# A two-layer hybrid model step on one core: where the output pieces stand in the linear-attention stage, and which engine copies its level products

## The chip, the cores and the metric

The kernel runs on one core of one Trainium2 chip. The metric is the device time of one execution in microseconds, from the first to the last instruction on the core and what lies around it. The engines are TensorE (PE, with its weight loads PEld), VectorE (DVE), ScalarE (ACT), GpSimd (POOL) and SyncE (SP), which issues most DMAs. All arithmetic here is in 32-bit floats.

## The reference

The model takes 1024 prompt tokens and 8 x 4 sample tokens through two layers. Each layer has a token mixer (pooling, latent attention and gated linear attention side by side, joined by `w_out`), cross attention, and a mixture of experts. The change touches the linear attention of the mixer, and the product with `w_out` that is begun beside it:

```python
def gla(q, k, v, log_a, s0):                       # 4 heads, DK 32, DV 64
    def step(S, inp):                              # one chunk of tokens
        qb, kb, vb, gb = inp
        b = jnp.cumsum(gb, axis=2)
        o_inter = jnp.einsum('bhtk,bhkv->bhtv', qb * jnp.exp(b), S)
        decay = jnp.exp(jnp.where(causal, b[:, :, :, None, :] - b[:, :, None, :, :], -jnp.inf))
        att = jnp.einsum('bhtsk,bhsk->bhts', qb[:, :, :, None, :] * decay, kb)
        o_intra = jnp.einsum('bhts,bhsv->bhtv', att, vb)
        S = jnp.exp(b_last)[..., None] * S + jnp.einsum('bhsk,bhsv->bhkv', kb * jnp.exp(b_last - b), vb)
        return S, o_inter + o_intra

y = jnp.concatenate([ya, yb, yc], axis=-1) @ lw['w_out']   # pooling, latent, linear attention
x = x + y
```

## The kernel before, in words

The program is written out by hand: every engine has its own list of instructions, and semaphores with counts order them. Each layer is a row of stages with a barrier (`stage_end`, L479) behind most. The third stage, "stage 3" here, is the linear attention: L1036 to L1141 on TensorE, L1723 to L1786 on ScalarE, L2210 to L2350 on VectorE, L2821 to L2856 on GpSimd. It stands once in each layer, behind the latent attention (stage 2), whose head pairs 0 to 3 use two weight slots `w_h` in turn.

Stage 3 works on 8 tiles of 128 tokens. Positions of a tile that are paired by the causal mask are split into 7 levels: at level z (64, 32, ..., 1) the first half of each block of 2z positions meets the second half. For tile n:

- VectorE `begin(n)` (L2219): a running sum of the log decays (L2225), then 7 subtractions (L2229), one for each level. There are two buffers, used in turn by even and odd tiles.
- ScalarE `decay_exps(n)` (L1726, L1727) takes exponentials of those, `state_exps(n)` (L1733 to L1735) those for the state.
- GpSimd multiplies them with q and k, 14 short products (L2834, L2836) and three longer (L2839, L2841, L2842). Count 2n+1 of `g_pool` stands for L2839, the last that the level products need.
- TensorE `levels(n)` (L1044, L1045): 28 small products into PSUM banks 0 to 3, one buffer only.
- VectorE `take_levels(n)`: 7 masked copies of them to the attention tile `g_att` (L2239), and a product for the diagonal (L2240), which counts `at_free`.
- TensorE `turn_kt` (L1051), `outputs` (L1058, L1060), `states` (L1067), and later `turn_o` (L1076) for the transposed outputs.
- VectorE `add_state` (L2261, a product with the mask of the 4 diagonal blocks, and L2262), `take_o` (L2247), `norm_o` for two tiles at a time (L2253, L2256, L2257).

Eight pieces of the product with `w_out` (`part(i)`, L1086: 6 contraction steps of 352 columns, in one PSUM bank, 5) are put between these on TensorE. VectorE adds each to x (`add_part`, L2269), and piece i + 1 waits for that (`part_or_counts_ready`). Their weights come in the four `ring` slots, which stage 2 uses for its probabilities, so that SyncE loads them behind the barrier. `keep_clock` (L760) issues products of constants that nothing reads. Behind the eight tiles the stage does the same for the 32 sample tokens (L2298 to L2345 on VectorE, L1112 to L1141 on TensorE).

Times in this section's stage are read from the execution's start: stage 3 begins at 423.97 us in layer 0 and at 1717.24 us in layer 1.

## Time and profile before

| | |
|---|---|
| median of 3 runs | 2597.96 us (2595.11 to 2601.43) |
| the profiled execution's own time | 2599.04 us |
| its span | 2597.2 us |
| PE busy | 2401.4 us, 92% |
| DVE busy | 1143.3 us, 44% |
| ACT busy | 689.8 us, 27% |
| POOL busy | 468.2 us, 18% |
| stage 3, layer 0 | 423.97 to 522.63 us |
| stage 3, layer 1 | 1717.24 to 1815.9 us |

A row of a timeline has the start in us, the duration in us, the engine, the line, the operation, what it writes and reads, and how many such instructions in a row it stands for; in brackets how long the engine sat idle before it, and what ended that. A duration of "x7" is that of all seven. A row of windows has the busy time and number of instructions of each engine in that stretch, then TensorE's granted clock as a share of 2.4 GHz, and the DMA load.

### The profile page before, as it was taken

How to read it: one execution, taken by the hardware profiler on the slowest of the kernel's cores; microseconds unless marked ns; L12 is line 12 of the kernel's file. 1: busy time of each engine (PE TensorE's matmuls, PEld its weight loads, DVE VectorE, ACT ScalarE, POOL GpSimd, SP SyncE). 2: the span in 40 equal slices, each digit the busy share in tenths (PEclk: the TensorE clock that was granted, in tenths of full speed). 3: DMA queues.
4: the chain of work that ended last, by engine and by line, in shares of the span. 5: the costliest groups of instructions: out<-in, count | busy, mean ns of one | idle time of the engine just before them, and what ended most of it. 6: DMA issues, size and time to landing. Idle time of an engine off the chain costs nothing.

```text
span 2597.2 us, 38234 instructions
## 1 busy us (share of the span) xinstructions
PE 2401.4 (92%) x15944; PEld 1422.5 (55%) x15944; DVE 1143.3 (44%) x2122; ACT 689.8 (27%) x1452; POOL 468.2 (18%) x566
## 2 busy tenths in 40 slices
PE   8999998899999999999899999888989999999984
PEld 5645556666666765333366445566666676733332
DVE  3355556843241445333253555568431433633334
ACT  1034444432111331111130344544321123311113
POOL 6004223410100001111260042243100000011112
PEclk9999999999999999999999999999999999999996
DMA  5001001152224228999840010011522421589996
GB/s 187 11 19 30 11 5 38 42 197 92 89 90 148 82 90 310 396 422 422 333 141 11 19 30 11 5 38 44 205 82 65 149 82 65 198 345 406 424 418 244
DMA packets 79220, 389.31 MB, mean 150 GB/s; under 512 B 20654, under 2 KB 24364, under 8 KB 59532
## 3 DMA queue, kind: packets, MB, share of 16 engines
q1 hardware_dynamic: 60892, 308.07, 31.1%
q0 software_dynamic: 17568, 76.57, 7.6%
q8 instruction: 131, 2.15, 0.3%
q10 hardware_dynamic: 576, 2.10, 0.2%
q14 instruction: 53, 0.43, 0.1%
HBM read 354.53 MB, written 41.41 MB: 152 GB/s over the span
## 4 chain that ended last, share of the span: by engine, by line
PE 73%; DVE 11%; ACT 4%; issue 4%; DMA 3%; PEld 2%; POOL 1%; POOLq 0%; PEldq 0%; SPq 0%; DVEq 0%; ACTq 0%
PE ps L1494 12%; PE ps L784 8%; PE ps L807 8%; PE ps L1518 6%; PE ps L1404 4%; PE ps L875 4%; PE ps L955 4%; PE ps L967 3%; PE ps L983 2%; PEld ps L807 2%; PE ps L1160 2%; PE ps L933 2%; DVE arena L2239 2%; PE ps L1480 2%; DMA arena<-yrow 1%
## 5 line engine op out<-in xcount | busy, mean ns | idle before, releaser
L1494 PE MATMUL ps<-arena 128*32 128x512 f32 x2304 | 319.6, 608 | 24.6 <-issue 18.9
L807 PE MATMUL ps<-arena,ring 128*128 128x352 f32 x936 | 283.2, 466 | 1.0 <-ACTq L481 1.0
L784 PE MATMUL ps<-x,ring 128*128 128x352 f32 x768 | 231.5, 463 | 10.6 <-DMA x<-in_x 9.1
L807 PEld LDWEIGHTS ps<-arena,ring 128*128 128x128 f32 x936 | 180.4, 193 | 101.9 <-issue 4.3
L2683 DVE COPY arena<-ps 128x1024 f32<-128x1024 f32 x44 | 53.9, 1224 | 336.9 <-PE ps L1480 336.9
L1494 PEld LDWEIGHTS ps<-arena 128*32 128x32 f32 x2304 | 92.7, 112 | 191.4 <-issue 191.4
L784 PEld LDWEIGHTS ps<-x,ring 128*128 128x128 f32 x768 | 146.8, 192 | 92.7 <-issue 12.8
L1518 PE MATMUL ps<-arena 128*32 128x512 f32 x1408 | 160.2, 595 | 3.8 <-ACT arena L1914 3.8
L2883 POOL DMA_INDIRECT arena<-xrow,arena x46 | 46.8, 1017 | 594.8 <-DVE arena L2658 321.3
L955 PE MATMUL ps<-arena 96*128 96x512 f32 (+3 forms) x384 | 148.7, 497 | 0.0
L1680 ACT ACTIVATE ring<-ps 128x512 f32<-128x512 f32 (+2 forms) x192 | 87.3, 490 | 128.7 <-PE ps L967 128.6
L1404 PE MATMUL ps<-arena,ring 128*128 128x352 f32 x384 | 117.7, 463 | 1.6 <-DVE arena L2516 1.6
L1160 PE MATMUL ps<-consts,arena 128*128 128x128 f32 x640 | 100.6, 297 | 18.9 <-ACT arena L1795 9.6
L875 PE MATMUL ps<-arena,x 128*128 128x512 f32 x256 | 114.5, 608 | 2.2 <-ACT arena L1628 2.2
L1494 PE MATMUL ps<-ring,arena 128*32 128x512 f32 x512 | 114.3, 600 | 0.0
L967 PE MATMUL ps<-consts,ring 128*128 128x128 f32 x576 | 91.4, 287 | 24.7 <-DVE arena L2151 9.7
L1685 ACT ACTIVATE ring<-ps,nmax 128x128 f32<-128x128 f32 (+7 forms) x128 | 94.5, 740 | 54.6 <-DVE nmax L2141 54.1
L1909 ACT ACTIVATE arena<-ps 128x256 f32<-128x256 f32 x44 | 16.9, 383 | 334.8 <-PE ps L1494 334.8
L2139 DVE TENSOR_TENSOR ps<-ps,consts 128x128 f32<-128x128 f32 x128 | 38.3, 299 | 150.2 <-PE ps L955 149.3
L1160 PEld LDWEIGHTS ps<-consts,arena 128*128 128x128 f32 x640 | 74.5, 150 | 48.9 <-ACT arena L1795 19.9
L2140 DVE TENSOR_REDUCE nmax<-ps 128x1 f32<-128x128 f32 (+7 forms) x128 | 97.0, 758 | 4.4
L967 PEld LDWEIGHTS ps<-consts,ring 128*128 128x128 f32 x576 | 65.6, 144 | 58.4 <-issue 35.1
(471 smaller groups left out, 3836.3 us busy)
## 6 DMA issues: line engine op xcount, KB each, us to landing
arena<-in_w_gu SPq DMA_DIRECT2D x52, 2048.0 KB, 14.3
arena<-in_w_dn SPq DMA_DIRECT2D x64, 1024.0 KB, 11.4
ring<-in_ring SPq DMA_DIRECT2D x56, 512.0 KB, 3.7
ring<-in_w_gu SPq DMA_DIRECT2D x12, 2048.0 KB, 13.7
arena<-yrow SPq DMA_DIRECT2D x16, 1024.0 KB, 9.3
arena<-in_mem_k SPq DMA_DIRECT2D x16, 512.0 KB, 7.6
arena<-in_mem_v SPq DMA_DIRECT2D x16, 512.0 KB, 9.5
xrow<-arena SPq DMA_DIRECT2D x16, 512.0 KB, 7.7
```

What stands on the lines that cost most here:

```text
L784: mm = pe.matmul(ps[:, PIECE_BANKS[n % len(PIECE_BANKS)], 0:CH], ring[:, j % RING, k, :], x[:, k, tok], start=k == 0, stop=k == KT - 1)
L807: mm = pe.matmul(ps[:, (j % 2) * NCH + c, 0:CH], ring[:, j // per, (j % per) * units + k, :], src[:, k, tok], start=k == k0, stop=k == uni ...
L875: mm = pe.matmul(ps[:, 6 + t % 2, :], x[:, k, t * P:t * P + m], wvg[:, k, :], start=k == 0, stop=k == KT - 1)
L955: mm = pe.matmul(ps[:, bank + at // 512, 0:end - at], q_h[0:QK, b, qb * P:(qb + 1) * P], k_h[0:QK, b, at:end], start=True, stop=True)
L967: mm = pe.transpose(ps[:, bank, (kb % 4) * P:(kb % 4 + 1) * P], prob[:, e, kb * P:(kb + 1) * P], ident)
L1160: mm = pe.transpose(ps[:, turn_bank(u), j * P:(j + 1) * P], b, ident)
L1404: mm = pe.matmul(ps[:, (j % 2) * NCH + c, 0:CH], ring[:, slot, (j % 2) * XH + k, :], co[:, k, tok], start=k == 0, stop=k == XH - 1)
L1494: mm = pe.matmul(ps[r, 2 + n % 2, :], xb_t[:, n % 2, k, r], w_gu[e % NW][:, k, :], start=k == 0, stop=k == KT - 1, skip_group_check=True)
L1518: mm = pe.matmul(ps[r, 4 + f, :], h_t[:, k, r], w_dn[e % NW][:, k, f * 512:(f + 1) * 512], start=k == 0, stop=k == 1, skip_group_check=True)
L1680: act.activation(pt[:, e, 512 * half:512 * half + w], ps[:, 4 + m % 2, 0:w], ACT.Copy).then_inc(tp_free[m % 2], 1)
L1685: act.activation(prob[:, e, 0:w], ps[:, 2 * e:2 * e + 2, :].rearrange("p a n -> p (a n)")[:, 0:w], ACT.Exp, bias=nmax[:, e, 1:2], scale=ML ...
L2140: step(dve.reduce_max(nmax[:, e, 0:1], sc, AX))
```

## The change

Four edits, all in stage 3.

1. **Pieces.** SyncE loads the weights of pieces 0 and 1 (both use the same block of `w_out`) during the last pair of stage 2, into the slot that pair 2 has left (`w_first`, a view of `w_h[0]`). TensorE does pieces 0 and 1 at the start of the stage in place of 10 `keep_clock` products, piece 2 behind `levels(0)`, and the rest behind tiles 0, 1, 2, 3 and 5. In place of piece 7 behind the tiles stand 16 `keep_clock` products; the 14 in tile 0 go.
2. **Levels.** Levels 64, 32 and 16 are copied by ScalarE with 7 unmasked copies, `keep_levels(n)`, which wait for `at_free` and count `at_kept`; VectorE keeps 4 masked copies. `levels` and `outputs` on TensorE wait for `at_kept` too.
3. **State.** The state product is written as 4 products of 32 x 64, one for each head, into diagonal blocks of a bank that VectorE has zeroed once; the masking product L2261 goes.
4. **Order.** VectorE does `begin(2)` ahead of the tiles, behind a wait for `g_pool`, and `add_part(0)` and `add_part(1)` behind it. GpSimd waits for `at_done` from tile 2 on.

```diff
@@ SyncE
+                sp.wait_ge(tp_done, SLOT[PAIRS - 2, ("a", 1, 0)] + 1)
+                sp.dma_start(w_first, ins["ring"][l, 2 * RING + PART[0][0]][:, 0:PART_K, :]).then_inc(w_full[0], 16)
@@ TensorE
                     if n >= 1:
                         pe.wait_ge(at_free, n)
+                        pe.wait_ge(at_kept, n)
...
-                    pe.matmul(ps[:, 7, 0:GW], g_ktt[:, n % 2, :], vg[:, n, 0:GW], start=True, stop=True).then_inc(st_done, 1)
+                    for h in range(GH):
+                        r, v = slice(GK * h, GK * (h + 1)), slice(GV * h, GV * (h + 1))
+                        mm = pe.matmul(ps[r, 7, v], g_ktt[:, n % 2, r], vg[:, n, v], start=True, stop=True)
+                    mm.then_inc(st_done, 1)
...
-                keep_clock(5, 10)
                 part(0)
+                part(1)
                 levels(0)
-                part(1)
+                part(2)
...
-                    if n == 0:
-                        pe.wait_ge(part_or_counts_ready, 2)
-                        keep_clock(5, 14)
-                    if 1 <= n <= len(PART) - 3:
-                        part(1 + n)
+                    if n in PART_AT:                       # (0, 1, 2, 3, 5)
+                        part(3 + PART_AT.index(n))
...
-                part(len(PART) - 1)
+                keep_clock(5, 16)
@@ ScalarE
+                def keep_levels(n):
+
+                    act.wait_ge(at_free, n + 1)
+                    for lv, z in enumerate(LEVELS[:HIGH]):
+                        for b in range(HALF // z):
+                            s_, at = 2 * z * b, lv * HALF + z * b
+                            last = act.activation(g_att[s_:s_ + z, n % 2, :, s_ + z:s_ + 2 * z], ps[s_:s_ + z, 0:GH, at:at + z], ACT.Copy)
+                            if at + z < HIGH * HALF:
+                                step.mark(last)
+                    last.then_inc(at_kept, 1)
...
+                decay_exps(2)
+                keep_levels(0)
                 for n in range(NT):
-                    if n + 2 < NT:
+                    if n >= 1 and n + 2 < NT:
                         decay_exps(n + 2)
...
+                    if n + 1 < NT:
+                        keep_levels(n + 1)
                     head_squares(n, P)
@@ VectorE
-                    for lv, z in enumerate(LEVELS):
+                    for lv, z in list(enumerate(LEVELS))[HIGH:]:
...
-                    step(dve.tensor_tensor(g_tmp, ps[:, bank, 0:GW], bd, ALU.mult))
-                    dve.scalar_tensor_tensor(out=dst, in0=dst, scalar=scale, in1=g_tmp, op0=ALU.mult, op1=ALU.add).then_inc(st_ready, 1)
+                    dve.scalar_tensor_tensor(out=dst, in0=dst, scalar=scale, in1=ps[:, bank, 0:GW], op0=ALU.mult, op1=ALU.add).then_inc(st_ready, 1)
...
+                step.mark(dve.memset(ps[:, 7, 0:GW], 0.0))
+                step.sync()
                 dve.memset(state, 0.0).then_inc(st_ready, 1)
                 begin(0)
-                begin(1)
                 step.mark(dve.memset(d_e[:, 2, :], 1.0))
                 step(dve.memset(g_att, 0.0))
+                begin(1)
+                dve.wait_ge(g_pool, 1)
+                begin(2)
                 add_part(0)
+                add_part(1)
...
-                add_part(len(PART) - 1)
@@ GpSimd
+                    if n >= 2:
+                        pool.wait_ge(at_done, n - 1)
                     pool.wait_ge(g_exp, 2 * n + 1)
```

How VectorE's list begins in stage 3, before (L2225 and L2229 are `begin`, L2269 is `add_part`, L2239 the first masked copy of tile 0; names in brackets are the semaphores waited for):

```order
L2271 MEMSET arena 128x256 [waits stage_done]
L2225 SCALAR_TENSOR_TENSOR arena<-arena 128x128
...
L2225 SCALAR_TENSOR_TENSOR arena<-arena 128x128
...
L2229 TENSOR_TENSOR arena<-arena 128x64x2
L2274 MEMSET arena 128x32
L2275 MEMSET arena 128x1024
L2269 TENSOR_TENSOR x<-x,ps 128x352 [waits part_or_table_done,dve_step]
L2239 COPY_PREDICATED arena<-lmask,ps 128x4x64 [waits at_done]
```

And now (L2248 and L2252 are `begin`, L2291 is `add_part`, L2262 the first masked copy):

```order
L2293 MEMSET ps 128x256 [waits stage_done]
L2295 MEMSET arena 128x256 [waits dve_step]
L2248 SCALAR_TENSOR_TENSOR arena<-arena 128x128
...
L2298 MEMSET arena 128x1024
L2248 SCALAR_TENSOR_TENSOR arena<-arena 128x128 [waits dve_step]
...
L2248 SCALAR_TENSOR_TENSOR arena<-arena 128x128 [waits g_exp,g_pool]
...
L2252 TENSOR_TENSOR arena<-arena 128x64x2
L2291 TENSOR_TENSOR x<-x,ps 128x352 [waits part_or_table_done] x2
L2262 COPY_PREDICATED arena<-lmask,ps 128x32x8 [waits at_done]
```

A third `begin`, with a wait for GpSimd, has moved in front of the addition of piece 0.

How TensorE's list begins in stage 3, before (L760 is `keep_clock`, L1086 a piece, L1044 and L1045 `levels`):

```order
L760 MATMUL ps<-consts 128x128 [waits stage_done]
L760 MATMUL ps<-consts 128x128 x9
L1086 MATMUL ps<-arena,ring 128x352 [waits ring_full1]
L1086 MATMUL ps<-arena,ring 128x352 x5
L1044 MATMUL ps<-arena 128x64 [waits g_pool,g_zero]
L1044 MATMUL ps<-arena 128x64 x27
L1045 MATMUL ps<-consts,arena 128x4
L1086 MATMUL ps<-arena,ring 128x352 [waits part_or_counts_ready,ring_full1]
```

And now (L1098 is a piece, L1049 and L1050 are `levels`):

```order
L1098 MATMUL ps<-arena 128x352 [waits pair_or_gu_full,stage_done]
L1098 MATMUL ps<-arena 128x352 x5
L1098 MATMUL ps<-arena 128x352 [waits part_or_counts_ready,pair_or_gu_full]
L1098 MATMUL ps<-arena 128x352 x5
L1049 MATMUL ps<-arena 128x64 [waits g_pool,g_zero]
L1049 MATMUL ps<-arena 128x64 x27
L1050 MATMUL ps<-consts,arena 128x4
L1098 MATMUL ps<-arena,ring 128x352 [waits part_or_counts_ready,ring_full2]
```

Piece 1, which waits for the addition of piece 0, has moved in front of the level products of tile 0.

ScalarE's list for one tile without square roots, now (L1735 and L1736 are `decay_exps`, L1748 `take_kt`, L1742 to L1744 `state_exps`, L1756 `keep_levels`, L1765 `head_squares`):

```order
L1735 ACTIVATE arena<-arena 128x7x64 [waits g_sub]
L1736 ACTIVATE arena<-arena 128x7x64
L1748 ACTIVATE arena<-ps 128x128 [waits kt_done]
L1742 ACTIVATE arena<-arena 128x128 [waits st_ready]
L1743 ACTIVATE arena<-arena 128x128
L1744 ACTIVATE arena<-arena 128x1
L1756 ACTIVATE arena<-ps 64x4x64 [waits at_free]
L1756 ACTIVATE arena<-ps 32x4x32 x2
L1756 ACTIVATE arena<-ps 16x4x16 x4
L1765 ACTIVATE arena<-arena 128x64 [waits o_evac]
```

Before, the list is the same without the three rows of L1756: they stand now behind the exponentials that wait for the state.

## Rows read from the trace of the kernel before

**Rows 1.** Windows: us, busy per engine, granted clock, DMA; tiles of layer 0.

```profile
434.51:500.71 66.20, 60.11 (x644) 47.43 (x644) 62.30 (x157) 27.00 (x106) 40.21 (x118) 1.00 0.08 29
```

**Rows 2.** Timeline, all engines, start of stage 3 in layer 0.

```profile
423.97 1.80 POOL L2821 MEMSET arena<- 128x2048 f32 x1 [53.25 <-DVEq L481]
424.09 0.27 DVE L2271 MEMSET arena<- 128x256 f32 x1 [0.23 <-DVEq L481]
...
427.56 0.47 POOL L2834 TENSOR_TENSOR arena<-arena 128x64 f32<-128x64 f32 x1
...
431.76 0.46 POOL L2839 TENSOR_TENSOR arena<-arena 128x128 f32<-128x128 f32 x1
...
432.37 1.79 PE L1044 MATMUL ps<-arena 32*128 32x64 f32 x56 [0.89 <-POOL arena L2839]
...
434.51 3.86 DVE L2239 COPY_PREDICATED arena<-lmask,ps 128x256 f32<-128x256 uint8 x7 [2.40 <-PE ps L1045]
```

**Rows 3.** Timeline, tile 1 to tile 2 of layer 0, and first copies of tiles 5, 6.

```profile
441.12 3.86 DVE L2239 COPY_PREDICATED arena<-lmask,ps 128x256 f32<-128x256 uint8 x7
442.08 0.90 DVE L2239 COPY_PREDICATED arena<-lmask,ps 128x256 f32<-128x256 uint8 x2
...
445.35 0.42 DVE L2261 TENSOR_TENSOR arena<-ps,consts 128x256 f32<-128x256 f32 x1
...
445.80 0.52 DVE L2262 SCALAR_TENSOR_TENSOR arena<-arena 128x256 f32<-128x256 f32 x1
...
446.35 0.31 ACT L1733 ACTIVATE arena<-arena 128x128 f32<-128x128 f32 x1 [3.88 <-DVE arena L2262]
...
446.57 0.41 DVE L2225 TENSOR_TENSOR_SCAN arena<-arena 128x128 f32<-128x128 f32 x1
...
446.95 0.24 ACT L1745 ACTIVATE arena<-arena 128x64 f32<-128x64 f32 x1
447.01 2.19 DVE L2229 TENSOR_TENSOR arena<-arena 128x128 f32<-128x128 f32 x7
...
447.28 1.79 PE L1044 MATMUL ps<-arena 32*128 32x64 f32 x56 [0.94 <-POOL arena L2839]
...
449.43 3.86 DVE L2239 COPY_PREDICATED arena<-lmask,ps 128x256 f32<-128x256 uint8 x7 [0.22 <-PE ps L1045]
...
449.82 1.00 PE L1060 MATMUL ps<-arena 128*128 128x64 f32 x8
...
451.15 3.71 PE L1086 MATMUL ps<-arena,ring 128*128 128x352 f32 x12
...
454.96 1.79 PE L1044 MATMUL ps<-arena 32*128 32x64 f32 x56
...
471.80 0.60 PE L1076 MATMUL ps<-consts,arena 128*128 128x128 f32 x4
...
476.19 3.83 DVE L2239 COPY_PREDICATED arena<-lmask,ps 128x256 f32<-128x256 uint8 x7
...
486.46 3.84 DVE L2239 COPY_PREDICATED arena<-lmask,ps 128x256 f32<-128x256 uint8 x7
```

**Rows 4.** Groups by line: busy us, mean ns of one; ScalarE's copies out of PSUM.

```profile
L1909 ACT ACTIVATE arena<-ps 128x256 f32<-128x256 f32 x44 | 16.9, 383 | 334.8 <-PE ps L1494 334.8
L1739 ACT ACTIVATE arena<-ps 128x128 f32<-128x128 f32 x8 | 2.1, 257 | 0.0
```

**Rows 5.** Windows of 1 us in stage 3 of layer 0; the clock stands third from last.

```profile
427.00:428.00 1.00, 1.00 (x9) 0.96 (x9) 1.00 (x6) 1.00 (x4) 0.87 (x3) 0.97 1.01 406
509.00:510.00 1.00, 0.69 (x2) 0.29 (x2) 0.93 (x4) 0.00 (x0) 0.00 (x0) 0.50 0.00 0
```

**Rows 6.** Timeline, tile 7 and what follows it, layer 0.

```profile
493.04 3.85 DVE L2239 COPY_PREDICATED arena<-lmask,ps 128x256 f32<-128x256 uint8 x7 [0.67 <-PE ps L1045]
...
500.71 0.42 DVE L2261 TENSOR_TENSOR arena<-ps,consts 128x256 f32<-128x256 f32 x1 [0.17 <-PE ps L1067]
...
507.60 0.84 PE L1114 MATMUL ps<-arena 128*32 128x128 f32 x6 [2.93 <-DVE arena L2321]
```

More of the change, by code:

```diff
@@ L106 @@
 PART = ((1, 1), (1, 0), (2, 0), (2, 1), (3, 0), (3, 1), (0, 0), (0, 1))
+PART_AT = (0, 1, 2, 3, 5)
 PART_K = 6
@@ L254, in build @@
         w_h = [view(SC + 4128, WP), view(SC + 256, WP)]
+        w_first = view(SC + 4128, PART_K, P)
         q_dec = view(SC, DB, ND)
@@ L271, in build @@
         la_t = view(SC + 3072 + TOK, TOK)
-        NL = len(LEVELS)
+        NL, HIGH = len(LEVELS), 3
         HALF = P // 2
@@ L388, in build @@
         g_sub, g_exp, g_pool, g_dve = sem("g_sub"), sem("g_exp"), sem("g_pool"), sem("g_dve")
-        at_done, at_free = sem("at_done"), sem("at_free")
+        at_done, at_free, at_kept = sem("at_done"), sem("at_free"), sem("at_kept_or_rx_in")
         kt_done, kt_evac, st_done, st_ready = sem("kt_done"), sem("kt_evac"), sem("st_done"), sem("st_ready")
@@ L407, in build @@
         wr_full, lg_done, lg_evac, lt_done = sem("wr_full"), sem("lg_done"), sem("lg_evac"), sem("lt_done")
-        rx_in, rx_out = sem("rx_in"), sem("rx_out")
+        rx_in, rx_out = at_kept, sem("rx_out")
         ranked, routed = sem("ranked"), sem("routed")
@@ L413, in build @@
         row_moved = [sem(f"row_moved{j}") for j in range(4)]
-        wg_full = [(sem(f"wg_full{j}"), 0) for j in range(4)] + [(w_full[0], 16 * PAIRS // 2)]
+        wg_full = [(sem(f"wg_full{j}"), 0) for j in range(4)] + [(w_full[0], 16 * (PAIRS // 2 + 1))]
         wd_full = [(s, 32 * PAIRS) for s in swap_or_dn_full] + [(w_full[1], 16 * PAIRS // 2)]
@@ L1050, in turn_kt @@
                     pe.wait_ge(st_ready, n + 1)
-                    pe.transpose(ps[:, 7, 0:P], g_kt[:, n % 2, :], ident).then_inc(kt_done, 1)
+                    pe.transpose(ps[:, 7, GW:GW + P], g_kt[:, n % 2, :], ident).then_inc(kt_done, 1)
                 def outputs(n):
                     pe.wait_ge(at_free, n + 1)
+                    pe.wait_ge(at_kept, n + 1)
                     if n >= 1:
@@ L1081, in part @@
                     j, c = PART[i]
-                    pe.wait_ge(ring_full[j], ring_count(l, 3))
+                    if i <= 1:
+                        pe.wait_ge(w_full[0], 16 * (PAIRS // 2 + 1))
+                    else:
+                        pe.wait_ge(ring_full[j], ring_count(l, 3))
                     if i >= 1:
@@ L1085, in part @@
                     for k in range(PART_K):
-                        mm = pe.matmul(ps[:, 5, 0:CH], ring[:, j, k, :], mix[:, k, chunks[c][1]], start=k == 0, stop=k == PART_K - 1)
+                        mm = pe.matmul(ps[:, 5, 0:CH], w_first[:, k, :] if i <= 1 else ring[:, j, k, :], mix[:, k, chunks[c][1]], start=k == 0, stop=k == PART_K - 1)
                     mm.then_inc(part_or_table_done, 1)
-                keep_clock(5, 10)
                 part(0)
+                part(1)
                 levels(0)
-                part(1)
+                part(2)
                 for n in range(NT):
@@ L1119, in _ @@
                 pe.wait_ge(st_ready, NT + 1)
-                pe.transpose(ps[0:ND, 7, 0:P], g_kt[:, 0, 0:ND], ident).then_inc(kt_done, 1)
+                pe.transpose(ps[0:ND, 7, GW:GW + P], g_kt[:, 0, 0:ND], ident).then_inc(kt_done, 1)
                 pe.wait_ge(ds_full, 16 * GH)
@@ L1900, in _ @@
                                    scale=rstd_t[0:m, t:t + 1]).then_inc(xr_evac, 1)
-                act.wait_ge(rx_in, 1)
+                act.wait_ge(rx_in, NT + 1)
                 act.activation(r_exp, r_exp, ACT.Exp).then_inc(rx_out, 1)
@@ L2213, in _ @@
                 hm = con("headmask").unsqueeze(2)
-                bd = con("bdmask")
                 def split(a, z):
@@ L2280, in _ @@
                     if n == 0:
-                        add_part(1)
+                        add_part(2)
                     if n >= 1:
@@ L2285, in _ @@
                         take_o(n - 1)
-                    if n + 2 < NT:
+                    if n >= 1 and n + 2 < NT:
                         begin(n + 2)
@@ L2290, in _ @@
                         norm_o(n - 2, P)
-                    if 2 <= n <= len(PART) - 2:
-                        add_part(n)
+                    if n - 1 in PART_AT:
+                        add_part(3 + PART_AT.index(n - 1))
                 dve.wait_ge(st_done, NT)
```

4 lines of the change are left out of this document (2 added, 2 removed).

## The prediction

> **What bounds the kernel now.** The page's busy shares say TensorE (92%), but they average over stages, and the change lies in one stage of each layer. So I read that stage. Over the eight tiles of layer 0, 66.20 us, VectorE is busy 62.30 us and TensorE 60.11 us [rows 1]: both are nearly full, and VectorE is the fuller. Next the timeline of two tiles. Tile 1's masked copies begin at 441.12, tile 2's at 449.43, 8.31 us later, and VectorE has sat idle only 0.22 us [rows 3]. Tiles 5 and 6, between which two tiles are normalised, lie 486.46 - 476.19 = 10.27 us apart with no idle time named [rows 3]. So the tiles run at VectorE's pace. Two others are close behind. On TensorE the level products of consecutive tiles, with a piece between, begin at 447.28 and 454.96: 7.68 us, and the latter with no wait in front [rows 3]. And those at 447.28 had waited 0.94 us for GpSimd. The start of the stage has another bound: a chain VectorE, ScalarE, GpSimd, TensorE that gives the first level products at 432.37, while piece 0 is done beside it [rows 2].
>
> I count from the stage's start, 423.97. T0 to T7 are the starts of VectorE's masked copies of each tile. Before: T0 = 434.51 - 423.97 = 10.54 [rows 2], T1 = 17.15, T5 = 52.22 and T6 = 62.49 [rows 3], T7 = 69.07, and the last state addition begins at 76.74 [rows 6].
>
> **The start: pieces 0 and 1, and begin(2).** The intended gain is that piece 0 needs no ring slot and takes the place of products that nobody reads. Those stood in time that TensorE had to wait anyway, for GpSimd's L2839 (ends 431.76 + 0.46 = 432.22, [rows 2]). What matters is the new order. TensorE now does piece 1 ahead of the level products of tile 0; piece 1 waits for the addition of piece 0; and VectorE does that behind begin(2), which waits for GpSimd's first tile. Step by step, from the stage's start:
> - A PSUM memset with its own wait comes ahead of begin(0). The like in the arena is 0.27 [rows 2]; with the wait I take 0.3.
> - GpSimd's tile 0 ran from 427.56 to 432.22, that is 3.59 to 8.25 [rows 2]. It shifts by 0.3. Begin(1) now lies beside its products, which slows some of them (the first is 0.47, with VectorE busy; the fourteen span 4.20 in all, 0.30 each): 0.4 to 0.8 more. I take 9.2.
> - begin(2): 0.41 + 2.19 = 2.6, the price beside a busy GpSimd [rows 3]: 11.8. The addition of piece 0, about 0.5 (as long as L2262, 0.52, [rows 3]): 12.3.
> - Piece 1 begins at 12.35. Piece 0 ended near 5.3 (its 3.71 [rows 3] and the slow clock of the first 3 us: the first window at 0.97 is that of 427, [rows 5]). TensorE has been idle for 7 us. After the idle 2.93 us in front of 507.60 [rows 6] and short work behind it the clock was 0.50 at 509 [rows 5]. So I expect 1.2 GHz for the first 3 us of piece 1 at least, which adds half of that, 1.5: piece 1 ends at 12.35 + 3.71 + 1.5 = 17.6.
> - The level products to the first copy took 434.51 - 432.37 = 2.14 [rows 2]: T0 = 19.7. That is 9.2 later than before. Bounds: 6.4 (GpSimd at 8.4, begin(2) at 1.9, full clock) and 10.6 (slower GpSimd, slow clock into the level products too).
>
> What hides here: the third begin and its exponentials are done, so nothing of tile 2 is late. Between T0 and T1 the order is copies, ScalarE, level products 1; before, 441.12 - 434.51 = 6.61. Now 2.9 + 1.2 + 2.2 = 6.3 with the prices below: 0.3 less. T1 = 26.0, before 17.15.
>
> **The levels.** Seven copies take 3.86; the fourth starts about 0.45 behind 442.08, at 442.53, so the first three, those that go, cost 1.41 and four cost 2.45 [rows 3]. The mask product goes too: 445.80 - 445.35 = 0.45 [rows 3]. VectorE saves 1.86 a tile, 14.9 over eight. If VectorE still set the pace, tiles would take 8.3 - 1.9 = 6.4, and with norms 10.3 - 1.9 = 8.4. But two bounds stop that.
>
> ScalarE's seven copies have no row here. The three shapes are 256, 128 and 64 elements out of PSUM. One of 256 is 0.383, one of 128 is 0.257 [rows 4]. Consecutive ScalarE instructions overlap by about 0.1 (0.31 starting at 446.35 and two more are over by 446.95, [rows 3]). Upper bound: 0.38 + 6 x 0.26 = 1.9 without overlap. Lower: 0.3 + 6 x 0.1 = 0.9. I take 1.2, near 0.28 + 2 x 0.16 + 4 x 0.14.
>
> The chain from tile to tile: copies 2.45, diagonal product to its end 0.45 (at_free at 2.9), state addition until 3.3, ScalarE's three exponentials 446.95 - 446.35 = 0.6 [rows 3] to 3.9, keep_levels 1.2 to 5.1, then level products to the next copy 449.43 - 447.28 = 2.15 [rows 3]: 7.3. It exists because keep_levels stands behind the exponentials that wait for the state, and the level products have one PSUM buffer.
>
> TensorE: with a piece in the tile 7.68, as before. The state product is 8 instructions of 64 columns instead of two of 256. The eight of this width in outputs take 1.00, from 449.82 to 450.82, and the state product then takes what is left until the piece at 451.15, some 0.3 to 0.5 [rows 3]. So it costs between nothing and 0.6 more. I take 0, since its products are 32 columns wide and one eighth of the size. The Trainium skill (TensorE: Matmul & The Clock Gate, Part 3: Packing small matmuls) says that products whose outputs start at different groups of 32 partitions run beside each other. No row here shows it for four groups; the upper bound of 0.6 in five tiles would make the sum 3 us a layer higher, the rule leaves it as it is.
>
> So tiles with a piece take 7.7: T1 to T3 15.4. T3 to T4 has norms and a piece to add: VectorE, 8.4 (10.27 - 1.86). T5 = T3 + 16.0 (TensorE 2 x 7.7 and 0.60 for the turned outputs, the row of 471.80, [rows 3]). T5 to T6, norms, no piece: 8.2. T6 to T7: TensorE has a piece and turned outputs behind its level products of tile 6: T7 = T5 + 15.6. Sum T1 to T7 47.0; before 51.92. So 4.9 is gained of the 11.2 that VectorE loses in six tiles. In T5 to T6 TensorE idles some 3 us without its piece; that may drop the clock, at a price of 0 to 1.5 in the tile behind: 0.7.
>
> T7 to the last state addition: before 500.71 - 493.04 = 7.67 [rows 6]. Now copies 1.4 shorter, but keep_levels(7) 1.2 in front of outputs(7), and keep_clock and the roots as before: 6.9, 0.8 less. Behind it, 16 constant products stand where piece 7 stood: TensorE waits for VectorE there anyway (2.93, [rows 6]). The addition of piece 7, behind which the last norms stood, goes: 0.4 less. The extra DMA of SyncE (weights of pieces 0 and 1) falls into stage 2, where nothing waits for it; it costs nothing; were it late, piece 0 would still come before GpSimd's first tile is done. The pool's wait for at_done of tile n - 2 is met long before; nothing.
>
> **Sum.** A layer: +9.2 - 0.3 - 4.9 + 0.7 - 0.8 - 0.4 = +3.5. Two layers: +7.0. The profiled execution, 2599.04, becomes 2606.0; it lies 1.1 above the median of the runs, whose sum would be 2605.0. I say 2605.5.
>
> At one more place the Trainium skill prices what I bounded: VectorE: DVE Perf Modes, The TRN2 errata, has a ScalarE copy out of PSUM at 172 cycles and one per element at 1.2 GHz, and ScalarE: Activation LUTs (What ACT_TABLE_LOAD costs) has consecutive ones overlap by about 93 ns. By that, an estimate, 128 elements are 0.25, where [rows 4] has 0.257, and the seven copies are 1.15. The sum would be 0.1 a layer lower.
>
> **Rivals.** A measurement of this kernel can tell 0.2%, 5.2 us, from no change.
>
> *The loss and the gain cancel (chance 0.20).* GpSimd's first tile is not slowed, begin(2) takes 1.9, the clock comes back early: T0 6.6 to 7.5 later, and the tiles gain 6. A layer +0.5 to +1.5, 2598 to 2602, say 2600. For it: in the first 3 us the chip came back to full clock within that time [rows 5]. Against: begin beside a busy GpSimd has been 2.6 each time.
>
> *ScalarE becomes the pace (0.18).* The seven copies cost nearer 1.9, on partial partitions, and stand behind table loads in even tiles; the chain from tile to tile is 8.0 to 8.3, and only 1 to 2 us of VectorE's saving is left. The clock is low in more tiles. A layer +6.5 to +8.5: 2613. For it: ScalarE's load in these tiles is only 27.00 of 66.20 [rows 1], so it is a matter of latency alone; against it the durations of [rows 4].
>
> *Faster (0.08).* VectorE sets the pace to the end: chain and TensorE overlap better than I have it, tiles take 6.4 and 8.4, the full 14.9 come off, against 9.2 at the start: -5.7 - 0.4 a layer, -12, 2587. It decides where the tiles with a piece fall below 7.0 us. Against it speaks TensorE's own 7.68 with no idle time [rows 3]; only fewer pieces in the tiles (five instead of six) speaks for it.
>
> The forecast itself has 0.54, with its own range of +2 to +5.5 a layer, 2602 to 2610. It covers 0.06 below 5.2 us of change. So slower by over 0.2% has 0.48 + 0.18 and some of the first rival's upper edge: 0.68; within 0.2% 0.23; faster 0.09. The range that leaves out no more than 2 in 10 goes from 2597.5 to 2614.
>
> **What would show it.** In the changed kernel's trace: piece 1 begins 11 to 13.5 us behind the stage's start, TensorE idle for 5 us or more in front of it, ended by the addition of piece 0; its granted clock at 0.50 there. First masked copy at 17 to 21 instead of 10.54. Tiles 1 to 3 apart by 7.3 to 8.0, TensorE without idle time or waiting for ScalarE's copies, VectorE with idle time in every tile. The last state addition 2 to 6 us later than 76.74. It would be wrong if piece 1 started before 9, or if tiles were apart by under 7, or if the time changed outside stage 3.

## The result and the profile after

The changed kernel takes 2610.05 us (median of 12 runs, 2603.2 to 2620.27), the kernel before 2597.22 on the same chip (12 runs, 2587.59 to 2603.88). The ratio is 1.0052, 95% interval 1.004 to 1.0064: 0.4 to 0.6% slower, some 13 us. The forecast was 2605.5, range 2597.5 to 2614. Direction and range held; the loss is 12.8, where the forecast stood for +7.5. One execution below, of e6_state_only, fell into a slow state (4095.66 us) and is left out.

First the page of the changed kernel: its span and the busy share of each engine.

```profile
span 2607.1 us, 38430 instructions
PE 2399.9 (92%) x16008; PEld 1423.2 (55%) x16008; DVE 1126.0 (43%) x2060; ACT 717.3 (28%) x1564; POOL 469.4 (18%) x566
```

VectorE has 17.3 us less to do than before (1143.3) and ScalarE 27.5 more (689.8); the span is longer all the same. So less work did not help; where it stands has to be looked at. Stage 3 of layer 0 now runs from 418.12 to 528.07, 109.95 us instead of 98.66; in layer 1 109.78 instead of 99.11 (in the kernel before that stage ends at 1816.35, where TensorE begins the next one, not at 1815.9).

The start of the stage on TensorE, changed kernel (timeline; against [rows 2]):

```profile
418.12 5.33 PE L1098 MATMUL ps<-arena 128*128 128x352 f32 x12 [1.53 <-DVEq L483]
430.66 5.87 PE L1098 MATMUL ps<-arena 128*128 128x352 f32 x12 [7.21 <-DVE x L2291]
436.46 1.79 PE L1049 MATMUL ps<-arena 32*128 32x64 f32 x56
...
443.45 1.80 PE L1049 MATMUL ps<-arena 32*128 32x64 f32 x56 [1.23 <-ACT arena L1756]
...
448.83 5.33 PE L1098 MATMUL ps<-arena,ring 128*128 128x352 f32 x12
454.10 1.79 PE L1049 MATMUL ps<-arena 32*128 32x64 f32 x56
```

Piece 0, then 7.21 us of nothing, ended by VectorE's addition (L2291), then piece 1, 5.87 instead of 3.7. The level products of tile 0 come only behind it, at 18.3 us from the stage's start; in [rows 2] they began at 8.4. VectorE's side of the same wait:

```profile
427.06 0.66 DVE L2248 TENSOR_TENSOR_SCAN arena<-arena 128x128 f32<-128x128 f32 x1 [2.32 <-POOL arena L2867]
427.75 2.41 DVE L2252 TENSOR_TENSOR arena<-arena 128x128 f32<-128x128 f32 x7
430.00 0.51 DVE L2291 TENSOR_TENSOR x<-x,ps 128x352 f32<-128x352 f32 x1
```

It sits idle for GpSimd, does begin(2), and only then adds piece 0, which had been ready since about 423.4.

The tiles on VectorE (first masked copy of tiles 0, 1, 2, then 5, 6, 7, and the last state addition; against [rows 3, 6]):

```profile
438.60 2.44 DVE L2262 COPY_PREDICATED arena<-lmask,ps 128x256 f32<-128x256 uint8 x4 [1.51 <-PE ps L1050]
445.80 2.41 DVE L2262 COPY_PREDICATED arena<-lmask,ps 128x256 f32<-128x256 uint8 x4 [3.03 <-PE ps L1050]
...
456.24 2.44 DVE L2262 COPY_PREDICATED arena<-lmask,ps 128x256 f32<-128x256 uint8 x4 [1.51 <-PE ps L1050]
...
480.93 2.43 DVE L2262 COPY_PREDICATED arena<-lmask,ps 128x256 f32<-128x256 uint8 x4 [1.45 <-PE ps L1050]
...
490.85 2.42 DVE L2262 COPY_PREDICATED arena<-lmask,ps 128x256 f32<-128x256 uint8 x4 [1.44 <-PE ps L1050]
...
501.39 2.42 DVE L2262 COPY_PREDICATED arena<-lmask,ps 128x256 f32<-128x256 uint8 x4 [1.95 <-PE ps L1050]
...
508.06 0.48 DVE L2284 SCALAR_TENSOR_TENSOR arena<-arena,ps 128x256 f32<-128x256 f32 x1 [1.06 <-PE ps L1075]
```

VectorE, which had no idle time to speak of in [rows 3], now waits for TensorE's level products in front of nearly every tile: it sets the pace no more. The tiles did not come closer for it: T1 to T2 is 10.44 (8.31 before), T5 to T6 9.92 (10.27), T6 to T7 10.54 (6.58). Windows of the changed kernel, where the granted clock stands third from last, show why two of these are long:

```profile
437.00:445.00 8.00, 6.77 (x117) 5.12 (x110) 3.36 (x7) 1.66 (x7) 4.38 (x15) 1.00 0.01 2
445.00:452.00 7.00, 7.00 (x37) 5.21 (x32) 5.72 (x15) 2.65 (x12) 1.08 (x2) 0.51 0.00 0
452.00:486.00 34.00, 28.95 (x356) 22.04 (x354) 26.73 (x68) 23.39 (x89) 20.88 (x66) 1.00 0.01 2
486.00:497.00 11.00, 9.97 (x84) 8.25 (x85) 6.81 (x18) 5.40 (x26) 7.23 (x21) 0.53 0.01 3
```

In [rows 1] the clock was 1.00 over all eight tiles. Here it is at half, 1.2 GHz, for 7 us around piece 3 and for some 10 us in tiles 5 and 6. Layer 1 of the kernel before was not free of it either: its clock fell once, for about 3.4 us in tile 1, and T1 to T2 took 8.74 there instead of 8.31:

```profile
1734.00:1738.00 4.00, 4.00 (x21) 3.64 (x19) 3.79 (x9) 1.21 (x3) 2.37 (x9) 0.57 0.00 0
```

Ahead of the changed kernel's second fall lies a gap, in the one tile without a piece; the timeline of TensorE there:

```profile
482.26 0.32 PE L1075 MATMUL ps<-arena 128*32 128x64 f32 x8
487.03 3.27 PE L1049 MATMUL ps<-arena 32*128 32x64 f32 x56 [4.45 <-ACT arena L1756]
...
493.88 5.00 PE L1098 MATMUL ps<-arena,ring 128*128 128x352 f32 x12
```

And the waits of the whole stage (engine and line, what it waited for: us in all, times, longest):

```profile
PE ps L1049 <- ACT arena L1756: 7.3, 5, 4.5
PE ps L1098 <- DVE x L2291: 7.2, 1, 7.2
```

ScalarE's seven copies, by form (busy us, mean ns of one), and in one tile behind the three exponentials:

```profile
L1756 ACT ACTIVATE arena<-ps 16x64 f32<-16x64 f32 x32 | 6.9, 214 | 0.8
L1756 ACT ACTIVATE arena<-ps 32x128 f32<-32x128 f32 x16 | 4.1, 259 | 0.2
L1756 ACT ACTIVATE arena<-ps 64x256 f32<-64x256 f32 x8 | 2.9, 364 | 11.3 <-DVE arena L2263 11.3
```

```profile
449.49 0.31 ACT L1742 ACTIVATE arena<-arena 128x128 f32<-128x128 f32 x1 [3.09 <-DVE arena L2284]
449.70 0.39 ACT L1743 ACTIVATE arena<-arena 128x128 f32<-128x128 f32 x1
450.00 0.19 ACT L1744 ACTIVATE arena<-arena 128x1 f32<-128x1 f32 x1
450.09 1.76 ACT L1756 ACTIVATE arena<-ps 64x256 f32<-64x256 f32 x7
```

The 128 and 256 forms cost what [rows 4] said (0.257 and 0.383), but the sum of the seven, 1.74, is also their time: they do not overlap, while the exponentials ahead of them do, by 0.1 (0.31 from 449.49, the next one starts at 449.70).

### The profile page after: what moved, and what is told of

It is laid out like the page before. It is cut to its first block, busy times and chain, and to the rows that moved or that the text cites. A ratio compares the mean times of both kernels' runs of the same rounds, so it can differ in the third digit from the quotient of the medians.

```text
span 2607.1 us, 38430 instructions
## 1 busy us (share of the span) xinstructions
PE 2399.9 (92%) x16008; PEld 1423.2 (55%) x16008; DVE 1126.0 (43%) x2060; ACT 717.3 (28%) x1564; POOL 469.4 (18%) x566
## 4 chain that ended last, share of the span: by engine, by line
PE 76%; DVE 10%; ACT 5%; issue 4%; PEld 2%; DMA 2%; PEldq 1%; POOL 1%; POOLq 0%; SPq 0%; DVEq 0%; ACTq 0%
PE ps L1503 12%; PE ps L788 9%; PE ps L811 8%; PE ps L1527 6%; PE ps L1413 4%; PE ps L879 4%; PE ps L959 4%; PE ps L971 2%; PE ps L987 2%; PE ps L1169 2%; PEld ps L811 2%; PE ps L937 2%; PE ps L1489 2%; PE ps L1098 1%; DVE nmax L2164 1%
## 5 line engine op out<-in xcount | busy, mean ns | idle before, releaser
L811 PEld LDWEIGHTS ps<-arena,ring 128*128 128x128 f32 x936 | 179.7, 192 | 101.3 <-issue 3.2
L788 PEld LDWEIGHTS ps<-x,ring 128*128 128x128 f32 x768 | 147.0, 192 | 92.9 <-issue 13.2
L1413 PEld LDWEIGHTS ps<-arena,ring 128*128 128x128 f32 x384 | 71.7, 190 | 46.1 <-issue 6.8
```

What stands on the lines that cost most here:

```text
L788: mm = pe.matmul(ps[:, PIECE_BANKS[n % len(PIECE_BANKS)], 0:CH], ring[:, j % RING, k, :], x[:, k, tok], start=k == 0, stop=k == KT - 1)
L811: mm = pe.matmul(ps[:, (j % 2) * NCH + c, 0:CH], ring[:, j // per, (j % per) * units + k, :], src[:, k, tok], start=k == k0, stop=k == uni ...
L1413: mm = pe.matmul(ps[:, (j % 2) * NCH + c, 0:CH], ring[:, slot, (j % 2) * XH + k, :], co[:, k, tok], start=k == 0, stop=k == XH - 1)
```

## The experiments

Stage 3 of both layers, from each kernel's one profiled execution; "rest" is the span without the two. The ratio is to runs of the kernel before on the same chip, whose medians were 2593.52 to 2597.22; compare kernels by the ratio first. A number behind T is a tile: T1 to T2 is the time from the first masked copy of tile 1 to that of tile 2.

| kernel | layer 0 | layer 1 | rest | median | ratio, 95% |
|---|---|---|---|---|---|
| before | 98.66 | 99.11 | 2399.4 | 2597.22 | |
| changed | 109.95 | 109.78 | 2387.4 | 2610.05 | 1.0052 (1.004 to 1.0064) |
| e1_add_first | 102.92 | 106.08 | 2397.4 | 2600.21 | 1.0012 (0.9993 to 1.003) |
| e2_kept_clock | 112.67 | 111.06 | 2395.7 | 2618.91 | 1.0087 (1.0061 to 1.0113) |
| e2b_kept_30 | 109.60 | 106.46 | 2395.0 | 2612.22 | 1.0072 (1.0048 to 1.0096) |
| e3_levels_dve | 110.07 | 110.06 | 2385.3 | 2607.32 | 1.0052 (1.0032 to 1.0071) |
| e4_keep_early | 109.01 | 109.35 | 2393.7 | 2615.27 | 1.0077 (1.0054 to 1.01) |
| e5_both | 100.65 | 100.80 | 2391.1 | 2598.33 | 1.001 (0.999 to 1.003) |
| e6_state_only | 96.66 | 95.64 | 2391.3 | 2588.48 | 0.9983 (0.9966 to 1.0) |
| e7_state_levels | 97.38 | 95.53 | 2388.5 | 2586.07 | 0.9971 (0.995 to 0.9991) |
| e8_fill_gap | 104.70 | 106.11 | 2384.9 | 2610.95 | 1.0059 (1.0038 to 1.008) |
| e11_one_a_tile | 93.98 | 93.95 | 2392.6 | 2583.06 | 0.9951 (0.9931 to 0.997) |
| e12_one_keep_early | 92.57 | 94.81 | 2403.3 | 2582.95 | 0.9942 (0.9922 to 0.9961) |
| e13_old_start_keep_early | 95.57 | 92.20 | 2394.4 | 2579.76 | 0.9925 (0.9901 to 0.995) |

The theory was: the new order at the start loses some 10 us a layer, and lowered clocks in the tiles eat what VectorE gains. The rival: the seven copies on ScalarE set a slower pace.

**e1_add_first**: the order at the start.

```diff
                 begin(1)
+                add_part(0)
                 dve.wait_ge(g_pool, 1)
                 begin(2)
-                add_part(0)
                 add_part(1)
```

> The changed kernel, with one line moved: VectorE adds piece 0 ahead of its wait for GpSimd and begin(2), not behind them. Theory (the new order makes TensorE wait 7 us for that addition): piece 1 begins some 6 us behind the stage's start instead of 12.5, without a slow clock; the first masked copy (T0) at about 12 us instead of 20.5, and the cold stretch in tile 1 goes with it. Stage 3 takes 99 to 102 us instead of 110.0, the kernel 16 to 22 us less than the changed one: equal to the kernel before within 0.2%. Rival (the stall is hidden by what follows; ScalarE's copies in the chain from tile to tile cost the 13 us): T0 comes earlier but the last state addition hardly moves; the kernel stays 8 us or more above the one before.

The time fell to 1.0012, which cannot be told from the kernel before, as expected. The way there was not: the first copy starts at 15.98, instead of 20.47 in the changed kernel and of the 12 expected, and piece 1, which begins at 7.11, is still slow:

```profile
434.20 6.80 PE L1098 MATMUL ps<-arena 128*128 128x352 f32 x12 [3.30 <-DVE x L2291]
```

So the position of one 0.51 us addition behind begin(2) costs some 4.5 us at the start of each layer, and the kernel 0.4%. The rest of the delay there is piece 1 itself, ahead of the level products. The fall of the clock in tile 1 is gone in layer 0 and still there in layer 1 (T1 to T2 7.94 and 10.71).

**e2_kept_clock** and **e2b_kept_30**: 60 or 30 constant products behind piece 0, so that TensorE stays busy in the gap.

```diff
                 part(0)
+                keep_clock(6, 60)
                 part(1)
```

> The changed kernel, with 60 products of constants (7 us) between piece 0 and piece 1, so that TensorE is not idle while it waits. It leaves the wait and takes away the slow clock that follows. If the clock is what costs: piece 1 takes 3.7 us instead of 5.87, and with the clock still up in tile 1 the stage is 4 to 5 us shorter in each layer, the kernel 8 to 10 us. If the wait itself costs (my theory): only the 2.1 us of piece 1 and perhaps the 2.5 us of tile 1 come back, T0 at 18.3, and the kernel stays 5 to 9 us above the one before.

> As e2 with 30 products of constants between pieces 0 and 1, about 7 us (60 took 13.56 us in e2 and pushed piece 1 back by 4.6 us). Clock alone: piece 1 begins where it does in the changed kernel (12.5 us behind the stage's start) and takes 3.7 us instead of 5.87: T0 at 18.3. If the 7.2 us of idle time are also what lets the clock fall in tile 1, both layers' T1 to T2 take 7.9 instead of 10.4: stage 3 4 to 5 us shorter, kernel 8 to 10 us less. If not (e2 had 10.7 in layer 0 and 7.94 in layer 1 there): 2 to 3 us a layer, kernel 4 to 6 us less than the changed one.

Neither is faster than the changed kernel; every branch of both expectations had them some 4 us or more below it. TensorE in e2_kept_clock, layer 0:

```profile
424.57 13.56 PE L764 MATMUL ps<-consts 128*128 128x128 f32 x120
437.97 3.71 PE L1098 MATMUL ps<-arena 128*128 128x352 f32 x12
...
453.63 5.75 PE L1098 MATMUL ps<-arena,ring 128*128 128x352 f32 x12
```

Piece 1 is back at 3.71, so its 5.87 was the clock. But 60 products last 13.56 us, not the 7 planned and longer than the gap, and the piece starts late, at 17.05. And the clock falls again around piece 3 (5.75) after 30 us in which TensorE was idle for 1.23 us at most: the later fall does not need a slow clock or a long gap before it. With 30 products (6.86 us) piece 1 begins at 12.56 as planned; it takes 5.48 in layer 0, behind 2.05 us of idle time, and 3.79 in layer 1, behind 0.36, and only in layer 1 does T1 to T2 stay at 7.94. Products that fill a gap are themselves in the way if they last longer than it.

**e3_levels_dve**: the changed kernel with all seven copies back on VectorE.

```diff
-        NL, HIGH = len(LEVELS), 3
+        NL, HIGH = len(LEVELS), 0
...
-                keep_levels(0)
```

> The changed kernel, with all seven levels copied by VectorE again; the order, the pieces and the state edit stay. Theory (sharing the levels gains nothing, since the chain through ScalarE and TensorE's pieces set the pace, and lets TensorE's clock fall): T0 stays near 20.5; T1 to T7 takes 47 to 50 us instead of 55.6 (VectorE's 51.9 of before less 0.45 a tile), and the clock stays up in the tiles. Stage 3 103 to 106 instead of 110, the kernel 6 to 14 us below the changed one. Rival (sharing is a gain that the start hides): the tiles get longer than 55.6 and the kernel slower than the changed one.

The same time as the changed kernel, and the same stage to 0.3 us a layer. With this order of pieces the sharing neither costs nor gains; the rival falls. What was expected fails too: the tiles did not get shorter (T1 to T7 56.17), and the clock fell in the same two places, so it is not the sharing that lets it fall. In this kernel, too, TensorE idles 4.29 us in the tile without a piece, there ended by GpSimd, and the level products behind it take 3.27.

**e4_keep_early**: ScalarE's copies ahead of the exponentials that wait for the state; **e5_both**: this and the order of e1.

```diff
+                    if n + 1 < NT:
+                        keep_levels(n + 1)
                     if n + 2 < NT:
                         state_exps(n + 2)
                     if n >= 2 and n % 2 == 0:
                         act.wait_ge(o_root, n // 2)
-                    if n + 1 < NT:
-                        keep_levels(n + 1)
```

> The changed kernel, with ScalarE's keep_levels(n+1) moved ahead of the exponentials that wait for the state. Theory (the copies stand in the chain from tile to tile, behind the state addition and the exponentials, and behind a second table load in even tiles): tiles bound by that chain get 1 us shorter, tile 5 to 6 some 2 us, TensorE's idle 4.45 us there becomes 2, its clock stays up and tile 6 to 7 gets 2 to 3 us shorter. Stage 3 takes 102 to 105 us instead of 110.0, the kernel 10 to 16 us less than the changed one. Rival (TensorE and its pieces set the pace of tiles, not ScalarE): under 2 us a layer.

> Both edits, the addition of piece 0 first and keep_levels early. If the stall at the start and the chain through ScalarE are separate costs they add up: stage 3 at 91 to 95 us against 98.7 before, the kernel 8 to 15 us below the one before (2583 to 2589). If they share a cost (the slow clock behind one of them is the same loss), the stage stays at 97 to 100 and the kernel within 0.2% of the one before.

e4 is not faster (1.0077; its interval overlaps that of the changed kernel), where 10 to 16 us less were expected. Tiles with a piece came 7.5 instead of 7.97 apart, but T5 to T6 stayed at 9.8, and T6 to T7 took 11.2 instead of 10.5:

```profile
490.57 3.26 PE L1049 MATMUL ps<-arena 32*128 32x64 f32 x56 [4.33 <-POOL arena L2867]
```

The gap remains, now ended by GpSimd: it seems that two chains of nearly one length end there, and taking one away shows the other. e5 is as e1 in time (1.001 against 1.0012), the second branch of its expectation; its stages, 100.7, are a little longer than the 97 to 100 named there.

**e6_state_only** and **e7_state_levels**: the kernel before with the new state product and addition (no mask product), and with these and the shared levels; pieces and start as before.

```diff
-                    pe.matmul(ps[:, 7, 0:GW], g_ktt[:, n % 2, :], vg[:, n, 0:GW], start=True, stop=True).then_inc(st_done, 1)
+                    for h in range(GH):
+                        r, v = slice(GK * h, GK * (h + 1)), slice(GV * h, GV * (h + 1))
+                        mm = pe.matmul(ps[r, 7, v], g_ktt[:, n % 2, r], vg[:, n, v], start=True, stop=True)
+                    mm.then_inc(st_done, 1)
```

> The kernel before with the state edit alone (four products of 32 x 64 into diagonal blocks of a zeroed bank, no masking product on VectorE). VectorE sets the pace there: 0.45 us less in each of eight tiles, less 0.3 for the memset and wait. Stage 3 95 to 96 us instead of 98.7, the kernel 5 to 7 us below the one before. Rival (TensorE's eight small products cost as much, or GpSimd's chain takes over): within 2 us.

> The kernel before with the state edit and the levels shared with ScalarE; its start, pieces and clock products stay. The chain copies, state addition, exponentials, ScalarE's copies (1.76), level products is 7.95 us, TensorE 7.7 with a piece: T1 to T7 48 to 50 us against 51.9. T0 stays at 10.9, but T1 comes 0.5 later. If the clock stays up (a piece in each tile 1 to 6): stage 3 95 to 97, kernel 3 to 7 us below the one before and not better than the state edit alone. If the clock falls in it too: stage 3 99 to 103, kernel above the one before; then sharing costs by itself, whatever the order at the start.

The state edit alone is at -0.17%, and its interval touches 1; the two together are a gain, 0.29%. What the sharing adds to the state edit cannot be told from nothing. In layer 0 of e7 the clock fell too (T2 to T3 10.71, against 7.96 in layer 1), and the kernel still gains. With the two parts alone the ratio is 0.9971, with the new pieces 1.0052. So the loss of the change comes with its pieces (their places, or the early weights), not with its arithmetic.

**e8_fill_gap**: 17 constant products in tile 4 of the changed kernel.

```diff
+                    if n == 4:
+                        pe.wait_ge(part_or_counts_ready, 7)
+                        keep_clock(5, 17)
```

> The changed kernel with 17 constant products (nobody reads them) in tile 4, the one tile without a piece. Theory, the gap lowers the clock: TensorE idles 4.45 us ahead of the level products of tile 5, which then take 3.27 instead of 1.79, and everything to piece 7 runs at 1.2 GHz. With the products in the gap the clock stays at 2.4 GHz: tile 5 to 6 about 8.4 us instead of 9.92, tile 6 to 7 about 8 instead of 10.54, the last state addition near 86 instead of 89.9 from the stage's start, 3.5 to 4.5 us a layer, time about 2602. Rival, ScalarE's table loads and GpSimd's late chain set these two tiles: both stay over 9.5 us and the time stays at 2608 to 2611.

In the trace the theory holds to 0.1 us: T5 to T6 8.42, T6 to T7 7.95 in layer 0, 8.41 and 7.96 in layer 1, at a clock of 1.00.

```profile
482.92 4.06 PE L764 MATMUL ps<-consts 128*128 128x128 f32 x34
487.45 1.79 PE L1049 MATMUL ps<-arena 32*128 32x64 f32 x56 [0.46 <-ACT arena L1759]
...
491.17 3.82 PE L1098 MATMUL ps<-arena,ring 128*128 128x352 f32 x12
```

The wait for ScalarE fell from 4.45 to 0.46: the products fill the gap and hold nothing up. The stages are 5.3 and 3.7 us shorter. But the median is 2610.95, as that of the changed kernel: the profiled execution (2597.53) was the fastest of eight, the other seven took 2605 to 2616. The gain of this trace does not show in the times. The fastest execution also had the highest granted clock of the eight, 0.967 on average, the others 0.962 to 0.966; whether the clock fell in tiles 5 and 6 of the others all the same, or they lost the gain elsewhere, is not in any trace.

**e11_one_a_tile**: free slot, shared levels and state product as in the change, its pieces laid out otherwise.

```diff
-PART_AT = (0, 1, 2, 3, 5)
+PART_AT = (0, 1, 2, 3, 4, 5)
...
                 part(0)
-                part(1)
+                keep_clock(6, 14)
                 levels(0)
-                part(2)
+                part(1)
...
-                        part(3 + PART_AT.index(n))
+                        part(2 + PART_AT.index(n))
...
                 begin(1)
+                add_part(0)
                 dve.wait_ge(g_pool, 1)
                 begin(2)
-                add_part(0)
-                add_part(1)
```

> The changed kernel (free slot, shared levels, new state product) with its pieces laid out otherwise: piece 0, 14 constant products, levels of tile 0, piece 1, then one piece in each of tiles 0 to 5; the addition of piece 0 stands ahead of the wait for GpSimd. Theory, the place of the pieces costs the changed kernel its gain: first masked copy at 11 to 13 us from the stage's start instead of 20.5, tiles about 8 us apart, the last state addition at 74 to 78, time 2584 to 2592, as of the kernel before with the state and level edits alone (2586.1) or a little under. Rival, the early weights and their DMA or the sharing itself cost something: the first copy stays beyond 15 and the time over 2596.

As expected: 2583.06, 0.49% under the kernel before, where the changed kernel is 0.52% over it. First copy at 11.91; T1 to T7 49.53 and 49.48, where the changed kernel took 55.59 and 55.45. TensorE at the start, and the window over the tiles:

```profile
432.25 3.29 PE L764 MATMUL ps<-consts 128*128 128x128 f32 x28
436.20 1.79 PE L1049 MATMUL ps<-arena 32*128 32x64 f32 x56 [0.66 <-POOL arena L2866]
...
438.17 3.80 PE L1098 MATMUL ps<-arena 128*128 128x352 f32 x12
```

```profile
439.04:495.56 56.52, 51.18 (x612) 38.66 (x611) 43.40 (x107) 36.01 (x143) 37.24 (x114) 1.00 0.01 2
```

The clock is 1.00 throughout. The first level products wait for GpSimd, those in the tiles for ScalarE's copies (0.41 to 0.81 us, 1.92 in front of tile 1). This separates the free slot, which is harmless, from the places of the pieces. Against e1, which has the addition of piece 0 in the same place, it is another 0.6%; it moves piece 1 behind the level products and puts a piece into tile 4 at once, and no run tells which of the two gives how much.

**e12_one_keep_early** and **e13_old_start_keep_early**: e11 and e7 with ScalarE's copies early, the edit of e4.

> As the kernel with one piece a tile, and ScalarE's copies of the next tile stand ahead of the exponentials that wait for the state. Theory, the chain from tile to tile through ScalarE binds in the tiles with a piece (TensorE waits 0.4 to 0.7 for it): tiles come 7.5 apart instead of 7.97, 2 to 3 us a layer, 4 to 5 us in all below it. Rival, TensorE's own work is 7.5 and VectorE then waits for the state: under 2 us in all.

> The kernel before with the state edit and the shared levels, its own pieces and start kept, and ScalarE's copies ahead of the exponentials. Theory, same as for the other early one: 0.4 us a tile, 2582 to 2584 against 2586.1 with the copies behind them. Rival, the state chain is delayed by as much: 2586 or more.

e12 is 2582.95, e11 2583.06: no gain that can be told, where 4 to 5 us were expected, though T1 to T7 is 46.7 in both layers. e13 is 2579.76, 0.75% under the kernel before, the best median of all; its interval (0.9901 to 0.995) meets those of e7, e11 and e12, so which of them is best is not settled. In e13, layer 1, the level products of consecutive tiles come 7.47 apart with no wait in front:

```profile
1742.54 1.79 PE L1045 MATMUL ps<-arena 32*128 32x64 f32 x56
...
1746.26 3.82 PE L1091 MATMUL ps<-arena,ring 128*128 128x352 f32 x12
1750.01 1.79 PE L1045 MATMUL ps<-arena 32*128 32x64 f32 x56
```

In these tiles TensorE is the bound at last. It was 7.68 in [rows 3].

## Why the prediction was right in sign and short in size

By its own steps, layer 0 (layer 1 in brackets), us a layer:

| step | forecast | measured |
|---|---|---|
| T0 | +9.2 | +9.93 (+9.84) |
| T0 to T1 | -0.3 | +0.59 (+0.69) |
| T1 to T7, with the clock's 0.7 | -4.2 | +3.67 (+3.01) |
| T7 to the last state addition | -0.8 | -1.00 (-1.01) |
| behind it | -0.4 | -1.90 (-1.86) |
| sum | +3.5 | +11.29 (+10.67) |

**The start** was right in mechanism and nearly in size: GpSimd's tile is done at 8.9 (9.2 forecast), begin(2) takes 2.9 (2.6), the addition of piece 0 ends the idle time, 12.54 us behind the stage's start (12.35), idle 7.21 (7), clock at half for about the first 4 us of piece 1. e1 shows the mechanism.

**T0 to T1**: ScalarE's copies were taken at 1.2 us and are 1.76 (bounds 0.9 to 1.9). The mistake was the overlap of 0.1 between consecutive instructions, read from three exponentials; the small copies out of PSUM follow each other every 0.25. The Trainium skill's overlap (ScalarE: Activation LUTs, What ACT_TABLE_LOAD costs) agrees with the trace for the exponentials, 0.1, but not for these copies. (The sum from its figures was also wrong: 1.64 less six overlaps of 0.093 is 1.09, not 1.15.) The chain's 7.3 became about 7.9, and TensorE waits 0.4 or more for it in tiles with a piece (e8, e11), 7.97 a tile instead of 7.7: 0.3 in each.

**T1 to T7** is the term that failed: 47.0 forecast (47.7 with the clock), 55.59 measured. Without any fall of the clock it is 49.5 (e11: shared levels, same order on ScalarE, and a piece in tile 4 too). So 2.5 is the slower chain against the 47.0 without the clock's part, and 6.1, as near as the traces tell, the clock against 0.7: T1 to T2 10.44 against 7.97, T5 to T6 9.92 against 8.42 (e8) and T6 to T7 10.54 against 7.95. I had named the gap in the tile without a piece, at some 3 us (measured 4.45), and priced it at 0.7; it cost 4.1. The error was to price it by its first 3 us of half clock, as at the start, while the clock stayed at half for some 10 us. The fall in T1 to T2 I had not foreseen. So two of the signs that I had named failed: tiles 1 and 2 are not 7.3 to 8.0 apart but 10.44, and the last state addition comes 13.2 us later, not 2 to 6. One term had an error the other way: the state product, taken as no dearer, is 0.24 cheaper from its start to that of the piece behind it (0.49 before, 0.25 now), and e13's 7.47 against 7.68 has room for that.

**The tail** gave 1.5 more than forecast. Piece 7 and its addition stood there; TensorE's idle time in front of the sample products is 2.33, by [rows 6] 2.93, and I had thought that wait all theirs. e6, which keeps piece 7 there, is 20.42 behind its last addition, e7 19.84; the changed kernel 20.02, the kernel before 21.46 counted in the same way (from its L2262). But layer 1 does not bear out that the state edit gives it: 21.39 before, 20.97 in e6, 21.59 in e7, 19.99 in the changed kernel. The shorter of these eight have the higher granted clock (0.84 in both layers before, 0.89 in both of the changed kernel; e6 0.89 and 0.83; e7 0.87 and 0.84). So the tail's length goes with the clock in it, and what the piece or the state edit gives by itself is not shown.

**The rivals**: "cancel" is out by the trace (+11). "ScalarE becomes the pace" named about the right time (2613) and in part the right signs, 1.76 a tile and a low clock in more tiles, but not the cause: with the copies on VectorE the time is the same (e3). "Faster" asked for tiles of 6.4; even in e13, layer 1, the level products come 7.47 apart. TensorE bounded it, as was said.

**Luck.** By the trace each stage lost three times the forecast, 11.0 us on average against 3.5. That the time still lies in the range, and at the edge of the narrower 2602 to 2610, is in part luck: outside the stage the changed kernel's trace is 12.0 us shorter, and the prediction has no term for that.

**What stays open.** The two stages together are 22.0 us longer in the profiled executions, the medians differ by 12.8. The rest of the program is the other way, 12.0 us shorter in the changed kernel's trace. I had written that a change outside stage 3 would prove me wrong. But its code there is the same but for one transfer, and over the fourteen traces the rest scatters from 2384.9 to 2403.3 with no order by edit; the kernel before lies near its upper end. Much of this scatter goes with the granted clock. The stretch ahead of stage 3 in layer 0, in the kernel before and in the changed one (clock third from last):

```profile
0.00:423.97 423.97, 391.10 (x1975) 233.69 (x1975) 203.39 (x399) 140.50 (x287) 104.24 (x75) 0.98 0.13 40
0.00:418.12 418.12, 385.29 (x1974) 230.43 (x1974) 203.58 (x399) 140.16 (x287) 104.55 (x75) 1.00 0.13 42
```

These are 5.85 of the 12.0 us; in e12 it took 427.30 at 0.97. The executions of one kernel show the same: of the changed kernel's twelve the shortest, 2603.2, had 0.966 on average, the longest, 2620.27, 0.959. So one trace a kernel carries 5 us or more of scatter, and whether the stage of the kernel before is usually longer than in its one trace, or something is really given back later, the runs do not tell. The same holds for e8.

## What to carry to other kernels

Before an instruction on the engine with time to spare is moved behind a wait, look for who waits for it: a half-microsecond addition behind another engine's first tile held up piece 1 on TensorE by 5.4 us (12.54 against 7.11 in e1). When work is taken from the engine that sets the pace, the next bound can be close by (here 8.3 to 7.97 to 7.47), and a TensorE that is then left with holes can lose its clock and with it more than was gained; spread the filler pieces so that each tile has one, as e11 does. Parts of one change should be run apart: here two together gained, and the third lost more than that. And one trace of each kernel is not enough to price a stage where the clock comes and goes.
